# A hybrid attention layer on one core: the first feed-forward projection as seven block products for eight

## Chip, cores and metric

One core of one Trainium2 chip. The metric is the device time in microseconds of one execution of the program.

## What is computed

One layer on x of 512 tokens by 1024, all in fp32:

```python
h = rms_norm(x, g_mix)
proj = h @ w_in                    # q, k, v of two attentions, two gates
ya = moba_attention(...)           # 8 heads, blocks of 256
yb = swa_attention(...)            # 8 query heads, window 128, sinks
merged = sigmoid(ga) * (ya @ w_branch_a) + sigmoid(gb) * (yb @ w_branch_b)
x = x + merged @ w_out
h2 = rms_norm(x, g_ffn)
x = x + square(relu(h2 @ w_ff1)) @ w_ff2
```

w_ff1 is 1024 x 4096 and w_ff2 is 4096 x 1024. The change concerns the last line.

## The kernel before

Every fp32 product is made from three matmuls in the type fp32r. A matrix is split into a high part (ScalarE copies it into fp32r) and a low part (the matrix less its high part, on POOL or VectorE); high x high, high x low and low x high are summed in PSUM (`products`, L1382 to L1390).

**Stages.** Weights come in slabs of 128 x 1024 (512 KB). g numbers them: 18 of the QKV projection, 16 of the gates (their matmuls stand between the steps of attention), 8 of the branch projections, 8 of the output projection, then 32 of w_ff1 and 32 of w_ff2. The attention has 32 steps of two units each. In a step VectorE takes the maxima, ScalarE the exponentials, VectorE the reciprocals (L1118), and POOL normalises (L554); TensorE transposes them two steps later (L1554).

**A slab's way.** SP loads it into one of RAW = 4 slots of `w_raw` (`load_slab`, L421) once the low part of the slab four before is made. ScalarE makes `w_hi` (`split_hi`, L624, L630) once TensorE has freed one of WS = 2 slots, POOL makes `w_lo` (`split_lo`, L535, L538), TensorE runs 8 x 3 matmuls of 512 columns (L1387 to L1389).

**Feed-forward stage.** The 4096 hidden columns go in 8 chunks (CHUNKS) of 512, so of four slabs of w_ff1 (TILES = 4). `up(j, c)` (L1691) makes one tile of 128 hidden columns by 512 tokens with 24 matmuls; ScalarE applies Relu (L823) and square (L829). The second projection of a chunk is already done in Strassen's way, with PRODUCTS = 7 block products for 8 (`product`, L1711; its matmuls are L1705, L1707, L1708, 12 of 512 columns each). Their weight operands are blocks of w_ff2 or sums of blocks: VectorE makes four sums per chunk (`weight_sum_1` to `weight_sum_4`, L1203 to L1222), ScalarE the seven high parts (`down_hi`, L831, L842), VectorE four of the low parts (L1237) and POOL three (L594). Their other operands are blocks of the squared tiles or sums of them (L1248 to L1259), split by ScalarE (L850) and VectorE (L1242). VectorE adds the products to sums in `store` (L1270, L1280).

**Order.** Each engine has a written-out order, in one loop over the chunks (PE L1742, ACT L919, DVE L1304, POOL L618, SP L508); semaphores with counts tie them. TensorE runs, in chunk c, tiles 1, 2, 3 of the chunk and tile 0 of chunk c+1, then products 0 to 6:

```python
with pe.Fori(0, CHUNKS - 2) as c:
    for j in range(1, TILES + 1):
        up(j, c)
    for k in range(PRODUCTS):
        product(k, c)
```

Chunks 6 and 7 are written out with the tiles of chunk 7 between the products of 6. SP loads four slabs of w_ff1 per chunk (L487) and reloads four blocks of w_ff2 (L493) when their readers are done. No DMA is issued by POOL, and ScalarE issues two, at the start.

## Time and profile before

| | |
|---|---|
| median of 3 runs | 675.34 us (674.37 to 676.03) |
| profiled execution | 674.49 us |
| its span | 672.7 us |
| PE, PEld busy | 99%, 82% |
| DVE, ACT, POOL busy | 75%, 55%, 48% |
| DMA | 69.87 MB, 104 GB/s |

The profile covers one execution. PE is TensorE's matmuls and PEld its weight loads, which overlap them; DVE is VectorE. The span is a little shorter than the measured time. A matmul's end in the records is modelled and overlaps the next one, so the distance between two starts, not the mean duration, is what one costs. Engines work side by side: time on an engine off the path does not show in the total.

### The profile page before, as it was taken

How to read it: one execution, taken by the hardware profiler on the slowest of the kernel's cores; microseconds unless marked ns; L12 is line 12 of the kernel's file. 1: busy time of each engine (PE TensorE's matmuls, PEld its weight loads, DVE VectorE, ACT ScalarE, POOL GpSimd, SP SyncE). 2: the span in 40 equal slices, each digit the busy share in tenths (PEclk: the TensorE clock that was granted, in tenths of full speed). 3: DMA queues.
4: the chain of work that ended last, by engine and by line, in shares of the span. 5: the costliest groups of instructions: out<-in, count | busy, mean ns of one | idle time of the engine just before them, and what ended most of it. 6: DMA issues, size and time to landing. Idle time of an engine off the chain costs nothing.

```text
span 672.7 us, 9474 instructions
## 1 busy us (share of the span) xinstructions
PE 668.1 (99%) x3238; PEld 553.8 (82%) x3238; DVE 502.2 (75%) x701; ACT 371.1 (55%) x662; POOL 322.8 (48%) x194
## 2 busy tenths in 40 slices
PE   9999999999999999999999999999999999999998
PEld 7887788888888888888888888888888888888886
DVE  6668898555555555875559879787897888979797
ACT  7468677776666666534357546253553625536360
POOL 0256577466555662444445536246452444436532
PEclk9999999999999999999999999999999999999999
DMA  8222342222233113454222322315132151230303
GB/s 322 95 98 91 86 138 71 73 79 94 95 95 95 64 53 109 167 181 179 88 71 94 129 90 85 133 62 174 57 108 96 62 187 62 94 108 18 126 0 126
DMA packets 22909, 69.87 MB, mean 104 GB/s; under 512 B 2731, under 2 KB 4011, under 8 KB 22876
## 3 DMA queue, kind: packets, MB, share of 16 engines
q1 hardware_dynamic: 22588, 68.92, 30.4%
q10 hardware_dynamic: 288, 0.52, 0.2%
q8 instruction: 19, 0.31, 0.2%
q14 instruction: 14, 0.11, 0.1%
HBM read 67.27 MB, written 2.16 MB: 103 GB/s over the span
## 4 chain that ended last, share of the span: by engine, by line
PE 97%; ACT 1%; DMA 1%; POOL 0%; issue 0%; DVE 0%; SPq 0%; ACTq 0%
PE bank L1387 21%; PE bank L1389 21%; PE bank L1388 21%; PE bank L1708 8%; PE bank L1707 8%; PE bank L1705 8%; PE bank L1488 3%; PE bank L1538 2%; PE bank L1554 2%; PE bank L1575 1%; PE bank L1577 1%; DMA store<-x_t 1%; PE bank L1677 1%; PE bank L1415 0%; PE bank L1416 0%; POOL w_lo L538 0%
## 5 line engine op out<-in xcount | busy, mean ns | idle before, releaser
L538 POOL TENSOR_TENSOR w_lo<-w_raw,w_hi 128x1024 fp32r<-128x1024 f32 x77 | 190.5, 2479 | 232.2 <-ACT w_hi L630 228.0
L1387 PE MATMUL bank<-qk_hi,w_hi 128*128 128x512 f32 x320 | 125.0, 391 | 0.0
L1389 PE MATMUL bank<-qk_hi,w_lo 128*128 128x512 f32 x320 | 124.5, 389 | 0.0
L1388 PE MATMUL bank<-qk_lo,w_hi 128*128 128x512 f32 x320 | 124.5, 389 | 0.0
L1387 PE MATMUL bank<-x_hi,w_hi 128*128 128x512 f32 x304 | 122.4, 402 | 0.1
L1389 PE MATMUL bank<-x_hi,w_lo 128*128 128x512 f32 x304 | 118.8, 391 | 0.0
L1388 PE MATMUL bank<-x_lo,w_hi 128*128 128x512 f32 x304 | 118.4, 390 | 0.0
L630 ACT ACTIVATE w_hi<-w_raw 128x1024 fp32r<-128x1024 f32 x80 | 83.9, 1058 | 57.3 <-PE bank L1389 53.2
L1270 DVE SCALAR_TENSOR_TENSOR store<-bank,softmax,store 128x512 f32<-128x512 f32 x101 | 71.9, 744 | 22.9 <-PE bank L1708 22.8
L1708 PE MATMUL bank<-v_parts,x_lo 128*128 128x512 f32 (+1 forms) x218 | 84.4, 387 | 0.0
L1705 PE MATMUL bank<-v_parts,x_hi 128*128 128x512 f32 (+1 forms) x218 | 84.4, 387 | 0.0
L1387 PEld LDWEIGHTS bank<-qk_hi,w_hi 128*128 128x128 f32 x320 | 60.1, 188 | 12.5 <-DVE w_lo L1181 0.2
L1389 PEld LDWEIGHTS bank<-qk_hi,w_lo 128*128 128x128 f32 x320 | 60.1, 188 | 12.5
L1388 PEld LDWEIGHTS bank<-qk_lo,w_hi 128*128 128x128 f32 x320 | 60.1, 188 | 12.3
L1389 PEld LDWEIGHTS bank<-x_hi,w_lo 128*128 128x128 f32 x304 | 57.0, 188 | 12.6
L1387 PEld LDWEIGHTS bank<-x_hi,w_hi 128*128 128x128 f32 x304 | 57.1, 188 | 12.0 <-issue 0.9
L1388 PEld LDWEIGHTS bank<-x_lo,w_hi 128*128 128x128 f32 x304 | 57.2, 188 | 10.8
L554 POOL TENSOR_SCALAR probs<-probs,softmax 128x256 f32<-128x256 f32 (+3 forms) x64 | 30.9, 495 | 58.4 <-DVE softmax L1118 58.3
L1123 DVE TENSOR_TENSOR pt_lo<-bank,pt_hi 128x256 fp32r<-128x256 f32 (+3 forms) x64 | 27.9, 439 | 36.6 <-ACT pt_hi L753 36.4
L842 ACT ACTIVATE v_parts<-qk_lo_again 128x1024 fp32r<-128x1024 f32 x21 | 21.5, 1057 | 57.1 <-DVE qk_lo_again L1213 45.9
L1705 PEld LDWEIGHTS bank<-v_parts,x_hi 128*128 128x128 f32 x218 | 40.9, 188 | 8.4
L1708 PEld LDWEIGHTS bank<-v_parts,x_lo 128*128 128x128 f32 x218 | 40.9, 188 | 8.3
(165 smaller groups left out, 1211.4 us busy)
## 6 DMA issues: line engine op xcount, KB each, us to landing
w_raw<-slabs SPq DMA_DIRECT2D x80, 512.0 KB, 3.3
bias_m<-slabs SPq DMA_DIRECT2D x16, 512.0 KB, 3.6
qk_hi_again<-slabs SPq DMA_DIRECT2D x16, 512.0 KB, 5.0
store<-x_t SPq DMA_DIRECT2D x16, 256.0 KB, 4.0
bias_m<-tab_dram SPq DMA_DIRECT2D x8, 256.0 KB, 4.2
out<-store SPq DMA_DIRECT2D x7, 256.0 KB, 2.8
bias_m<-tab_dram SPq DMA_DIRECT2D x8, 128.0 KB, 3.9
w_raw<-slabs ACTq DMA_DIRECT2D x2, 256.0 KB, 3.4
```

What stands on the lines that cost most here:

```text
L538: pool.tensor_tensor(w_lo[:, g % WS, :], w_raw[:, g % RAW, :], w_hi[:, g % WS, :].bitcast(F32), ALU.subtract).then_inc(w_lo_ready, 1)
L554: pool.tensor_scalar(probs[:, u % 4, 0:n], probs[:, u % 4, 0:n], rec[:, u % 8:u % 8 + 1], 1.0, ALU.mult, ALU.mult).then_inc(probs_ready, 1)
L630: act.activation(w_hi[:, g % WS, :], w_raw[:, g % RAW, :], ACT.Copy).then_inc(w_hi_ready, 1)
L842: act.activation(high, from_, ACT.Copy).then_inc(unit_hi_ready, 1)
L1123: dve.tensor_tensor(pt_lo[:, slot(u), keys], bank[5 + e][:, keys], pt_hi[:, slot(u), keys].bitcast(F32), ALU.subtract).then_inc(pt_lo_read ...
L1270: dve.scalar_tensor_tensor(out=to, in0=product, scalar=factor(j, m), in1=to, op0=ALU.mult, op1=ALU.add).then_inc(ready, 1)
L1387: pe.matmul(out_, wh, xh, start=first, stop=False)
L1388: pe.matmul(out_, wh, xl, start=False, stop=False)
L1389: last = pe.matmul(out_, wl, xh, start=False, stop=end)
L1705: pe.matmul(to, u_high, high[:, p, cols], start=(opens and p == 0), stop=False, skip_group_check=True)
L1707: pe.matmul(to, u_high, low[:, p, cols], start=False, stop=False, skip_group_check=True)
L1708: last = pe.matmul(to, u_low, high[:, p, cols], start=False, stop=(p == 1), skip_group_check=True)
```

## The change

Chunk 0's up projection stays as it was (three tiles after the one before). In chunks 1 to 7 the product of w_ff1's 1024 x 512 part with the 512 tokens is done as a 2 x 2 block product in Strassen's way (Winograd's form), with seven block products (UPS). The contraction is halved into even and odd tiles, the tokens into two halves (NEAR, FAR), the hidden columns into two halves. One block product is 2 x 4 x 3 = 24 matmuls of 256 columns.

- **Token operands.** While the output projection runs, ScalarE scales x1 (`scaled_x1`), VectorE makes four sums of half tiles per pair of tiles (`half_sums`), and both split them into `sum_hi` and `store_low`. They serve all chunks.
- **Weight sums.** The sums of weight blocks for both projections are made in DRAM (`sum_dram`): a DMA copies a block (28 issued by ACT, 32 by SP), and accumulating DMAs issued by POOL add another block or sum. There are 15 sets (chunk and projection) of four sums: 60 copies and 60 accumulating DMAs of 512 KB. The copies are issued from the QKV stage on; one accumulating DMA per step of attention, then two per slab. VectorE's weight sums go, and SP loads seven blocks per projection and chunk for four.
- **Low parts.** Of the seven up blocks, four low parts are made by POOL (0, 4, 5, 6); for blocks 1, 2, 3 (ADDED_UPS) ScalarE writes the negated high part and an accumulating DMA from POOL adds the fp32 block to it. Of the down products VectorE makes 1, 2, 3 and POOL 0, 4, 5, 6.
- **Order.** TensorE runs the seven up blocks of chunk c and then its products in the order 0, 2, 1, 3, 4, 5, 6; nothing of chunk c+1 stands ahead of them. For the last chunk the up blocks stand between products 4 and 5 of the chunk before.
- **After a block.** The blocks add up in banks 7 and 6 in part, and in SBUF in part: VectorE adds banks to tiles (`up_product`, five per chunk), ScalarE copies block 0 out (`first_up_copy`), and applies Relu and square to four results.

Core of the diff (the rest follows from it: counts of semaphores, slots, host arrangement of w_ff1):

```diff
+SUM_ORDER = [(SETS[n - back], s) for n in range(len(SETS) + 1) for back, s in ((0, S1), (1, S2), (0, S3), (1, S4))
+             if 0 <= n - back < len(SETS)]
...
# SP
+            def copy_down(n):
+                at, s = COPY_DOWNS[n]
+                sp.dma_start(set_at(at)[s], block_of(at, COPIED["down"][s])).then_inc(copy_done[at], 16)
...
                 load_slab(g)
+                if 0 <= g - COPIES_BEHIND < len(COPY_DOWNS):
+                    copy_down(g - COPIES_BEHIND)
...
+            for c in range(CHUNKS):
+                more = c + 1 < CHUNKS
+                if c == 0:
+                    sp.wait_ge(slab_done, G_FF + TILES)
+                    for k in (4, 5):
+                        load_up(k, 1)
+                if more:
+                    next_down(3, c)
+                    next_down(2, c)
+                if c and more:
+                    next_up(0, c)
+                if c:
+                    sp.wait_ge(up_done, up_count(1, c))
+                    load_up(6, c)
+                sp.wait_ge(b_lo_ready, c * len(B_UNITS) + 1)
+                load_down(6, c)
+                if more:
+                    next_down(1, c)
+                if c and more:
+                    for k in (2, 3, 4, 5, 1):
+                        next_up(k, c)
+                if more:
+                    next_down(4, c)
+                    next_down(5, c)
+                    next_down(0, c)
...
# POOL
+            def add_to_sum(n):
+                if n >= len(SUM_ORDER):
+                    return
+                at, s = SUM_ORDER[n]
+                if s in (S1, S3):
+                    pool.wait_ge(copy_done[at], 64 if at == ("up", 1) else 128)
+                    src = block_of(at, ADDED[at[0]][s])
+                else:
+                    pool.wait_ge(sum_done[at], 32 if s == S2 else 48)
+                    src = set_at(at)[S1 if s == S2 else S2]
+                pool.dma_start(set_at(at)[s], src, accum_op=ALU.add,
+                               max_dma_last_dim=4 * D).then_inc(sum_done[at], 16)
...
+                if step >= 1:
+                    add_to_sum(step - 1)
...
-            for g in range(LATE + 2, G_FF + 3):
+            for g in range(LATE + 2, G_FF + TILES):
                 split_lo(g, g + 3)
+                for n in range(2):
+                    add_to_sum(STEPS + 2 * (g - LATE - 2) + n)
...
+            def up_add(k, c):
+                at = ("up", c)
+                src = block_of(at, UP_BLOCK[k]) if k in UP_BLOCK else set_at(at)[UP_SUM[k]]
+                pool.wait_ge(up_minus_ready, (c - 1) * len(ADDED_UPS) + ADDED_UPS.index(k) + 1)
+                pool.dma_start(w_low[:, RAW_SLOT[k], :], src, accum_op=ALU.add).then_inc(up_added[k], 16)
...
                 down_lo(0, c)
+                if c:
+                    for k in (4, 5, 6):
+                        up_lo(k, c)
+                up_lo(0, c + 1)
+                down_lo(4, c)
...
+                    down_lo(5, c)
+                    up_add(2, c + 1)
+                    down_lo(6, c)
+                    up_add(1, c + 1)
+                    up_add(3, c + 1)
...
# ACT
             for g in range(N_VA, N_QKV):
                 split_hi(g + 2)
+                copy_up(g - N_VA)
...
+            def chunk(c):
+                down_hi(3, c)
+                down_hi(2, c)
                 down_hi(0, c)
                 down_hi(1, c)
+                first_up_copy(c)
+                up_hi(4, c)
+                up_hi(5, c)
+                up_relu(0, c)
+                up_square(0, c)
+                up_hi(6, c)
+                u_part_hi(6, c)
+                up_hi(0, c + 1)
+                up_relu(1, c)
+                up_square(1, c)
+                u_part_hi(0, c)
+                up_relu(2, c)
+                up_square(2, c)
+                u_part_hi(2, c)
+                up_relu(3, c)
+                up_square(3, c)
+                u_part_hi(1, c)
+                u_part_hi(3, c)
+                down_hi(4, c)
+                u_part_hi(4, c)
+                u_part_hi(5, c)
+                next_splits(c)
...
# DVE
+            def chunk_start(c):
+                for k in T_UNITS:
+                    down_lo(k, c)
+                up_product(1, c)
+                up_product(3, c)
+                u_part_lo(6, c)
+                up_product(4, c)
+                up_product(5, c)
+                u_part_lo(0, c)
+                u_sum_1(c)
+                up_product(6, c)
+                u_sum_2(c)
+                u_part_lo(2, c)
+                u_part_lo(1, c)
+                add_both(0, c)
+                u_sum_3(c)
+                u_part_lo(3, c)
+                u_sum_4(c)
+                u_part_lo(4, c)
+                add_both(2, c)
+                add_both(1, c)
+                u_part_lo(5, c)
+                add_both(3, c)
+                add_both(4, c)
...
# PE, in up(k, c)
+                for n in range(2):
+                    to = out_[:, S // 2 * n:S // 2 * n + S // 2]
+                    for i in range(KT // 2):
+                        high, low = up_weight(k, i, n)
+                        x_high, x_low = up_moving(k, i)
+                        pe.matmul(to, high, x_high, start=(k in UP_OPENS and n == 0 and i == 0), stop=False,
+                                  skip_group_check=True)
+                        pe.matmul(to, high, x_low, start=False, stop=False, skip_group_check=True)
+                        last = pe.matmul(to, low, x_high, start=False, stop=(i == KT // 2 - 1), skip_group_check=True)
...
-            with pe.Fori(0, CHUNKS - 2) as c:
-                for j in range(1, TILES + 1):
-                    up(j, c)
-                for k in range(PRODUCTS):
+            with pe.Fori(1, CHUNKS - 2) as c:
+                ups(c)
+                for k in ORDER:
                     product(k, c)
```

## Rows read from the trace of the kernel before

**Rows 1.** The page: span, busy time of each engine, the chain that ended last.

```profile
span 672.7 us, 9474 instructions
PE   668.1 (99%) x3238; PEld 553.8 (82%) x3238; DVE 502.2 (75%) x701; ACT 371.1 (55%) x662; POOL 322.8 (48%) x194
...
PE 97%; ACT 1%; DMA 1%; POOL 0%; issue 0%; DVE 0%; SPq 0%; ACTq 0%
```

**Rows 2.** Busy time by stretch, with granted clock, DMA share and GB/s.

```profile
core 0: us, PE busy (x) PEld busy (x) DVE busy (x) ACT busy (x) POOL busy (x), PEclk, DMA share, GB/s
0.00:25.00 25.00, 23.78 (x103) 20.22 (x104) 17.41 (x33) 16.10 (x23) 2.21 (x8) 1.00 0.73 259
25.00:120.00 95.00, 95.00 (x433) 76.92 (x433) 75.50 (x92) 66.49 (x114) 58.38 (x30) 1.00 0.30 95
...
433.00:474.00 41.00, 41.00 (x183) 33.95 (x182) 34.35 (x34) 19.47 (x26) 18.76 (x7) 1.00 0.30 102
```

**Rows 3.** Timeline of VectorE, one chunk apart: start, duration, instruction.

```profile
430.12 0.75 DVE L1270 SCALAR_TENSOR_TENSOR store<-bank,softmax,store 128x512 f32<-128x512 f32 x1 [0.61 <-PE bank L1708]
...
470.92 0.75 DVE L1270 SCALAR_TENSOR_TENSOR store<-bank,softmax,store 128x512 f32<-128x512 f32 x1 [0.61 <-PE bank L1708]
```

**Rows 4.** Timeline of the end of the kernel, PE, PEld and DVE.

```profile
664.07 0.39 PE L1707 MATMUL bank<-pt_hi,x_hi 128*128 128x512 f32 x1
...
667.69 0.39 PE L1708 MATMUL bank<-v_parts,x_lo 128*128 128x512 f32 x1
...
667.92 0.28 PE L1705 MATMUL bank<-v_parts,x_hi 128*128 128x256 f32 x1
...
668.03 0.28 PE L1707 MATMUL bank<-v_parts,x_hi 128*128 128x256 f32 x1
668.04 0.19 PEld L1708 LDWEIGHTS bank<-v_parts,x_lo 128*128 128x128 f32 x1
...
669.23 0.28 PE L1708 MATMUL bank<-v_parts,x_lo 128*128 128x256 f32 x1
669.55 0.48 DVE L1377 SCALAR_TENSOR_TENSOR store<-bank,softmax,store 128x256 f32<-128x256 f32 x1 [0.16 <-PE bank L1708]
```

**Rows 5.** Groups of instructions by form, 390 to 630 us: busy, mean ns.

```profile
L630 ACT ACTIVATE w_hi<-w_raw 128x1024 fp32r<-128x1024 f32 x24 | 24.6, 1051 | 0.0
L1237 DVE TENSOR_TENSOR pt_hi<-qk_lo_again,v_parts 128x1024 fp32r<-128x1024 f32 x18 | 21.4, 1218 | 7.3 <-ACT v_parts L842 7.3
L1222 DVE TENSOR_TENSOR qk_lo_again<-qk_hi_again,qk_lo_again 128x1024 f32<-128x1024 f32 x6 | 20.5, 3422 | 0.0
L594 POOL TENSOR_TENSOR pt_hi<-qk_hi_again,v_parts 128x1024 fp32r<-128x1024 f32 x6 | 20.4, 3402 | 0.0
L594 POOL TENSOR_TENSOR v_parts<-bias_m,v_parts 128x1024 fp32r<-128x1024 f32 x6 | 14.4, 2399 | 26.5 <-ACT v_parts L842 26.5
L1242 DVE TENSOR_TENSOR x_lo<-probs,x_hi 128x512 fp32r<-128x512 f32 x24 | 29.2, 1236 | 0.0
L823 ACT ACTIVATE probs<-bank 128x512 f32<-128x512 f32 x24 | 14.3, 594 | 16.8 <-PE bank L1389 16.7
L1280 DVE TENSOR_TENSOR pt_lo_again<-bank,pt_lo_again 128x512 f32<-128x512 f32 x12 | 7.7, 683 | 0.0
L1213 DVE TENSOR_TENSOR qk_lo_again<-qk_hi_again,qk_lo_again 128x1024 f32<-128x1024 f32 x6 | 7.4, 1226 | 0.3
L1217 DVE TENSOR_TENSOR bias_m<-qk_hi_again,bias_m 128x1024 f32<-128x1024 f32 x6 | 7.3, 1219 | 0.0
L1207 DVE TENSOR_TENSOR qk_lo_again<-bias_m 128x1024 f32<-128x1024 f32 x6 | 7.3, 1217 | 0.0
```

**Rows 6.** Timeline of a chunk, VectorE and then ScalarE.

```profile
449.61 0.69 DVE L1257 TENSOR_TENSOR x_lo_again<-probs 128x512 f32<-128x512 f32 x1
...
450.34 0.64 ACT L850 ACTIVATE x_hi<-x_lo_again 128x512 fp32r<-128x512 f32 x1 [2.63 <-DVE x_lo_again L1257]
```

**Rows 7.** The page: DMA queue (share of 16 engines) and issues with time to landing.

```profile
q1 hardware_dynamic: 22588, 68.92, 30.4%
...
w_raw<-slabs SPq DMA_DIRECT2D x80, 512.0 KB, 3.3
bias_m<-slabs SPq DMA_DIRECT2D x16, 512.0 KB, 3.6
qk_hi_again<-slabs SPq DMA_DIRECT2D x16, 512.0 KB, 5.0
```

**Rows 8.** Tile w_raw: ns of one DMA issue (min/median/max) on SP and ACT.

```profile
L429 SPq DMA_DIRECT2D w_raw<-slabs x55: 327/328/517, 7.2 to 352.3; - x55
...
L412 ACTq DMA_DIRECT2D w_raw<-slabs x1: 413/413/413, 0.7 to 0.7; - x1
```

**Rows 9.** Timeline of a slab of the output stage: ScalarE, POOL, TensorE.

```profile
312.58 1.06 ACT L630 ACTIVATE w_hi<-w_raw 128x1024 fp32r<-128x1024 f32 x1 [3.63 <-PE bank L1389]
...
313.72 2.40 POOL L538 TENSOR_TENSOR w_lo<-w_raw,w_hi 128x1024 fp32r<-128x1024 f32 x1 [3.53 <-ACT w_hi L630]
...
318.58 0.48 PE L1387 MATMUL bank<-x_hi,w_hi 128*128 128x512 f32 x1
```

**Rows 10.** Waits: who waited for whom, us in total, times, longest.

```profile
POOL probs L554 <- DVE softmax L1118: 58.3, 23, 5.0
```

**Rows 11.** Busy time by stretch, two slabs of the output stage.

```profile
312.67:318.58 5.91, 5.91 (x31) 4.90 (x30) 3.07 (x3) 2.16 (x4) 2.40 (x1) 1.00 0.49 180
...
324.51:330.43 5.92, 5.92 (x32) 4.90 (x30) 3.08 (x3) 2.17 (x4) 2.40 (x1) 1.00 0.27 94
```

More of the change, by code:

```diff
@@ L616, in last_lows @@
                 down_lo(5, c)
-            with pool.Fori(0, CHUNKS - 1) as c:
+            for c in range(CHUNKS - 1):
                 chunk_lows(c)
@@ new lines, in relu, with square, up_hi @@
+            def relu(j):
+                act.wait_ge(slab_done, G_FF + j + 1)
+                act.activation(u_raw[:, j, :], bank[7 - j % 2][:, :], ACT.Relu).then_inc(relu_ready, 1)
+            def square(j):
+                act.wait_ge(relu_ready, j + 1)
+                u = u_raw[:, j, :]
+                act.activation(u, u, ACT.Square).then_inc(u_ready, 1)
+            def up_hi(k, c):
+                slot = RAW_SLOT[k]
+                if k < 4:
+                    if isinstance(c, int) and c == 1:
+                        act.wait_ge(slab_done, G_FF + TILES)
+                    else:
+                        act.wait_ge(up_done, up_count((4, 5, 6, 3)[k], c - 1))
+                else:
+                    act.wait_ge(up_done, up_count(k - 4, c))
+                act.wait_ge(up_arrived[slot], up_arrived_count(k, c))
+                act.activation(quarters(up_high[HIGH_SLOT[k]]), up_raw(slot), ACT.Copy).then_inc(up_hi_ready, 1)
@@ L1699, in product_part, with ups @@
+            def ups(c):
+                for k in range(UPS):
+                    up(k, c)
             def product_part(k, m, out_, high, low, cols, opens):
```

628 lines of the change are left out of this document (404 added, 224 removed).

## The prediction

> **What bounds the kernel now.** I read the page's first part and its chain first [rows 1]: TensorE is busy 99% of a 672.7 us span, and 97% of the chain that ended last is matmul. The profiled execution took 674.49 us, 1.8 us more than its span and 0.85 us less than the median of the three runs (675.34), so my sums are made against 674.5 and 0.85 us is added at the end. Then the windows by stage [rows 2]: in a chunk of the feed-forward stage VectorE works 34.4 of 41 us, ScalarE 19.5, POOL 18.8 and the DMA engines are 30% busy. The clock is granted in full (1.00, the 2.4 GHz level) in every stretch. The timeline of the chunk loop [rows 3] gives the period: the same VectorE addition starts at 430.12 and at 470.92, 40.80 us apart. A chunk has 96 matmuls of the up projection and 84 of the down products; 40.80/180 = 0.2267 us each, which is the distance of back-to-back 512-column matmuls at the end of the kernel [rows 4], where 664.07 to 667.69 is 16 of them. So the loop has no PE gap at all: any PE time taken out shows in full, as long as nothing else becomes late, and nothing that relieves another engine pays anything.
>
> **What the change takes out.** Chunks 1 to 7 lose 7 x 96 = 672 matmuls of 512 columns and gain 7 blocks x 24 = 168 matmuls of 256 columns each, 1176. The price of one with 256 columns stands in the last product of the kernel [rows 4]: from 668.03 to 669.23 are ten steps, 0.120 us, not the half of 0.2267 (0.113). The weight load (0.19 us there as elsewhere) overlaps the matmuls before it and does not stretch this. Removed: 672 x 0.2267 = 152.3 us. Added: 1176 x 0.120 = 141.1 us; with the 0.119 that the whole group gives (667.92 to 669.23 in 11 steps), 140.1. I take **11.7 us less** PE time. 674.5 - 11.7 = 662.8.
>
> The Trainium skill (TensorE: Matmul & The Clock Gate, Back-to-back issue gap) gives the gap as columns over 2.4 GHz plus 2.5 ns, that is 109 and 216 ns. By that page the exchange would be 145.0 against 128.4 us and save 16.6. The trace has 120 and 227 ns for this kernel's operands, so the rows decide.
>
> **What must stay hidden in a chunk.** The new period is 40.80 - 1.67 = 39.1 us.
> - ScalarE: before, 11 copies of 1024 elements and 15 passes of 512, at 1.05 and 0.6 us [rows 5]; after, 17 and 16, about 28 of 39.1 us. Hidden.
> - VectorE: the four weight sums go (1.22 + 1.23 + 1.22 + 3.42 = 7.1 us) and one of four low parts (1.2); five additions from PSUM come (5 x 0.69) [rows 5]. 34.4 - 8.3 + 3.5 = 29.6. Hidden, and worth nothing by itself.
> - POOL: eight subtractions for seven, 2.4 us alone and up to 3.4 when VectorE is in its way [rows 5], and three accumulating DMAs. At most 27 us plus the issues. Hidden on average.
> - DMA: 17 transfers of 512 KB for eight. In the first 25 us the engines are 73% busy at 259 GB/s [rows 2], so full use is 355 GB/s and 512 KB cost 1.5 us of all 16: 25 us of 39.1, up to 30 if an accumulating one costs double. Busy, not full.
>
> **Latencies at the chunk's start.** Before, the first tile of chunk c+1 stood ahead of the products of chunk c (24 x 0.2267 = 5.4 us of cover). Now products follow the seven blocks at once. Product 0 needs only block 4. Product 2, second in the new order, needs block 5: let block 5 end at 0. VectorE starts 0.2 us after a matmul's successor could (669.23 + 0.12 to 669.55 [rows 4]); hops between engines are 0.05 (449.61 + 0.69 to 450.34 [rows 6]). Addition 0.9, Relu 1.5, square 2.2, S1 2.9, its high part 3.6. VectorE has meanwhile queued block 6's addition, which waits for that block (2.86): 3.75, then S2: 4.5, then the low part of S1: 5.2. PE wants it after block 6 and product 0, at 2.86 + 2.72 = 5.58. It fits by 0.4 us. Product 1 (its parts ready at about 6.5, wanted at 8.3) and product 3 fit by more. Block 2's wait for the copy of block 0 out of its bank has 2.86 us for a 0.6 us copy. I put these at nothing, with up to 0.5 us a chunk (3.5 in all) as the upper end. PE takes its work in order, so a miss is a gap.
> The queues of a chunk: SP loads the raw block 6 once block 1 has freed its slot, at 5.7, so that it lands at 9 to 10.7 (3.3 to 5.0 us [rows 7]); its two parts take 1.05 and up to 3.4 us, and PE wants them at 17.2. POOL issues the accumulating DMA of the next block 1 behind the low part of product 6, at about 35 us of 39.1; block 1 is wanted 2.9 us into the next chunk, at 42.0, so it may take 6.6 us. Both are hidden.
>
> **The weight sums in DRAM.** This is the part that no row of before shows. 60 copies and 60 accumulating DMAs of 512 KB are added, and with 66 more loads in the feed-forward stage the traffic grows by 186 x 1.5 = 279 us of all engines, to 204 (30.4% of the span [rows 7]) + 279 = 483 of 660; doubled accumulates (81) make it about 600. The queues:
> - Issue on ACT costs 0.42 us, on SP 0.33 [rows 8]. ACT: 14 in the QKV stage, one per 5.4 us slab, where it idles 30%, and 14 in attention, one per two steps. Hidden. SP's 32 copies stand between slab loads, each loaded up to four slabs ahead and landing in 3.3 us [rows 7]; a copy ahead of it adds some 1.5 to 3 us. Hidden.
> - Issue on POOL has no row: nothing to 1.7 us, the latter being half of the 3.5 us that POOL idles per slab in the output stage [rows 9]; beyond it PE waits. I take about 1 us, nearer ACT's row than the end. In attention POOL waited 58 us for VectorE's reciprocals, 2.5 us a time [rows 10], and the issue stands there. Hidden; up to 1 us in total is allowed where it isn't.
> - Landing time of an accumulate: from 3.3 us (a load [rows 7]) to about 8 (5.0, the slowest row for 512 KB, and a second read at 1.5, doubled by traffic). POOL itself waits for the one two places earlier. In attention two places are two steps, over 10 us. From the branch stage on there are two per slab, so POOL may wait once an accumulate needs more than a slab's 5.4 to 5.9 us. What stands behind that wait is the low part of the slab weights, ready only 2.5 us before PE takes it (313.72 + 2.40 against 318.58 [rows 9]). I take 4.8 us, one load and one more read: hidden.
> - The extra ScalarE and VectorE work in the output stage (eight scaled copies, twelve sums) goes into 3.5 us idle per slab on ScalarE [rows 9]. Nothing.
>
> The sum: 662.8, plus 1.4 for small gaps (0.2 us in each of seven chunks, under half of the bound) = 664.2; plus 0.85 for the median: **665.0**. A measurement of this kernel can tell about 0.3%, 2 us, from no change.
>
> **Rivals.**
> 1. *The accumulates in DRAM are late (slower).* The place is the 16 slabs of the branch and output stages and the first up tiles. Per slab the engines have 0.27 to 0.49 of 5.92 us in use already [rows 11]; two accumulates at 1.5 us bring that to 4.6 to 5.9, at 3.0 us (reading both terms) to 7.6 to 8.9. It decides from 5.9 us a slab and makes the kernel slower than before (677.4, the 0.3% included) from 6.8. At 7.0 it costs 1.1 x 16 = 18 us: 662.8 + 0.85 + 18 = 682; at 6.5 half of that, 673. For it: the sums leave no slack once doubled. Against: loads share the engines with the POOL queue, and slab loads land four slabs ahead. Chance 0.27 that it is slower by this.
> 2. *The shared port makes the new chain miss (gain partly lost).* One VectorE subtraction of 1024 took 3.42 us beside POOL's, and 1.23 alone; one of 512 from the u tiles 1.24 on average instead of 0.68 [rows 5]. If a POOL subtraction lies over the 5.2 us chain, product 2 is 2.0 us late, in seven chunks 14 us: 678, a bit slower; if it does so only in part, 0.5 to 1 us a chunk, 667 to 671. Against: by the order on POOL its next-chunk subtraction ends before block 5 does and the following one waits for product 0. Chance 0.15, most of it for the partial case.
> The Trainium skill (SBUF — State Buffer, SBUF: two separate sides) calls this an exclusive lock held for a whole instruction, with DMA descriptors from POOL shut out as well. The trace agrees for POOL's subtractions; no row of before has a DMA from POOL.
> 3. *The copies saturate the DMA engines in the QKV stage,* so slabs and bias tiles come late at the start of attention: 24 copies in 76 us make 36 us on top of 30% (23 us), 78% in use; at double price for writing DRAM, 125%. Then some 5 to 10 us are lost there, 670 to 675. Chance 0.08.
> 4. Forecast, all of it hidden but for 3 us: chance 0.50.
>
> **Numbers.** The likeliest case gives 665, its own range 662.5 to 668. The other cases reach upward: the range is 662 to 682. Faster by over 0.3% takes the forecast, most of 3 and the partial part of 2: 0.63. Within 0.3%: 0.10. Slower: 0.27.
>
> **What would show it.** Right: up blocks of 24 matmuls in 2.86 us, a chunk period of 39.1, no PE idle before the up blocks or products, stages before the feed-forward stage ending when they did. Rival 1: PE idle before slab matmuls released by POOL's w_lo in the branch and output stages, and POOL waiting for a DMA. Rival 2: PE idle before product 2 released by VectorE's x_lo. Rival 3: gaps before 200 us behind a load. The forecast is wrong if the 256-column step is over 0.13 us, since 0.01 us more costs 12 us.

## The result, and the profile after

The changed kernel takes 735.63 us (median of 4 runs, 734.69 to 736.81) against 675.68 for the kernel before on the same chip: ratio **1.0885** (95% interval 1.0866 to 1.0903), 60 us slower. The forecast was 665.0, faster, and its range ended at 682. The profiled execution has a span of 732.8 us.

The page of the kernel after: span, engines, TensorE clock and DMA in 40 slices of 18.3 us, queues (packets, MB, share of 16 engines), the chain that ended last.

```profile
span 732.8 us, 10654 instructions
PE 682.2 (93%) x3742; PEld 581.0 (79%) x3742; DVE 480.9 (66%) x719; ACT 426.7 (58%) x723; POOL 401.8 (55%) x282
...
PEclk9999999997999999989899999999999999999799
DMA  8487698999999997999997677593949577585503
...
q1 hardware_dynamic: 35468, 109.29, 42.4%
q0 software_dynamic: 11664, 42.47, 31.0%
q10 hardware_dynamic: 1184, 15.21, 5.3%
...
PE 41%; DMA 31%; POOL 12%; DVE 7%; ACT 4%; issue 4%; DVEq 0%; ACTq 0%; SPq 0%
```

Against [rows 1] the chain has left TensorE: it was 97% PE, it is 41%, and 31% is DMA. The DMA digits of the slices 6 to 21 are 8 and 9 but for one. Queue 0 is POOL's: it carries the 81 accumulating DMAs (60 in DRAM, 21 into SBUF) and nothing else. 0.310 x 732.8 / 81 = **2.8 us of all 16 engines each**. A transfer in q1 (109.29 MB are 208 of 512 KB, loads and SP's 32 copies) costs 0.424 x 732.8 / 208 = 1.49, and q10, ScalarE's queue, carries 28 copies at 0.053 x 732.8 / 28 = 1.39.

Busy time by stretch (PE, PEld, DVE, ACT, POOL, then granted clock, DMA share of 16 engines, GB/s), kernel after:

```profile
25.00:120.00 95.00, 95.00 (x428) 76.83 (x429) 75.24 (x93) 66.13 (x114) 60.14 (x31) 1.00 0.76 260
120.00:290.00 170.00, 157.47 (x942) 130.04 (x941) 87.23 (x263) 100.05 (x269) 108.50 (x120) 0.97 1.00 268
290.00:345.00 55.00, 47.02 (x195) 37.69 (x194) 29.16 (x29) 21.33 (x29) 30.32 (x24) 0.94 1.04 256
345.00:392.00 47.00, 40.93 (x177) 32.97 (x176) 26.73 (x28) 22.16 (x31) 22.16 (x17) 0.93 1.02 235
433.00:474.00 41.00, 40.29 (x256) 36.26 (x255) 32.46 (x34) 26.12 (x33) 23.55 (x11) 1.00 0.68 208
```

The QKV stage (25 to 120) has the DMA engines at 0.76, where [rows 2] had 0.30, and still no PE gap. From 120 to 392 they are full (1.00 to 1.04), and PE idles 12.5, 8.0 and 6.1 us. These 26.6 us are not the whole loss: the granted clock in the three rows is 0.97, 0.94 and 0.93, so up to 0.03 x 170 + 0.06 x 55 + 0.07 x 47 = 11.7 us more lie in matmuls that ran at the lower level (1.2 GHz) after gaps. The last row is 41 us of the feed-forward loop, a little over one chunk, against the 433 to 474 of [rows 2]: VectorE down, ScalarE and POOL up, and 0.7 us of PE idle.

The waits of the kernel after (who waited for whom: us in total, times, longest), then the group of POOL's issues that stand behind them, then from the page the issues with their time to landing:

```profile
POOL sum_dram L712 <- DMA sum_dram<-sum_dram: 84.9, 14, 9.0
...
PE bank L1725 <- POOL w_lo L676: 25.5, 14, 4.9
PE bank L2072 <- DMA w_raw<-sum_dram: 6.7, 6, 2.4
PE bank L2089 <- DVE pt_lo_again L1576: 4.5, 1, 4.5
```

```profile
L712 POOL DMA_DIRECT2D sum_dram<-sum_dram x30 | 31.2, 1041 | 86.8 <-DMA sum_dram<-sum_dram 84.9
```

```profile
w_raw_again<-slabs SPq DMA_DIRECT2D x66, 512.0 KB, 6.6
...
sum_dram<-slabs POOLq DMA_DIRECT2D x30, 512.0 KB, 10.9
sum_dram<-sum_dram POOLq DMA_DIRECT2D x30, 512.0 KB, 10.5
```

POOL waits 84.9 us for its own accumulates, which land 10.5 to 10.9 us after issue (medians of the whole run; 12.4 and 12.7 for those issued in attention, from 120 to 255 us). The low part of the slab weights (L676) stands behind that wait, and PE behind the low part. A weight load that took 3.3 us [rows 7] now takes 6.6. POOL's timeline in the output stage shows it in one place (start, duration, instruction, idle before and its releaser):

```profile
300.62 0.80 POOL L712 DMA_DIRECT2D sum_dram<-slabs  x1
307.43 0.83 POOL L712 DMA_DIRECT2D sum_dram<-sum_dram  x1 [6.00 <-DMA sum_dram<-sum_dram]
307.97 2.66 POOL L676 TENSOR_TENSOR w_lo<-w_raw_again,w_hi 128x1024 fp32r<-128x1024 f32 x1
```

and PE takes that low part up 2.77 us late:

```profile
310.69 0.64 PE L1725 MATMUL bank<-qk_hi,w_hi 128*128 128x512 f32 x1 [2.77 <-POOL w_lo L676]
```

It is the same everywhere: each of PE's 15 gaps between 140 and 400 us comes 1 to 5 us after the end of one of POOL's 14 waits for a landing.

**Where the 60 us are.** Starts of matmuls in the trace, in us after the kernel's first matmul; e1 is the first experiment, without the sums in DRAM:

| | before | after | e1 |
|---|---|---|---|
| last scores of attention | 236.7 | 253.0 | 238.0 |
| first transpose ahead of the feed-forward slabs | 305.5 | 333.7 | 306.9 |
| last of these transposes | 347.3 | 385.8 | 348.6 |
| first product of chunk 0 | 369.2 | 408.0 | 365.1 |
| last product | 668.1 | 728.6 | 686.2 |

Against e1, 42.9 us are lost ahead of the first product (15 in attention, 12 more by the first transpose, so in the branch stage and the first two slabs of the output stage, 10 in the rest of the output stage, 6 in the slabs after it). The feed-forward stage itself is no shorter than before. By blocks: chunk 0's products take 26.5 us instead of 19.0, the seven up blocks of chunks 1 to 6 take 21.0 to 21.4 where 168 steps of 0.120 are 20.15, the last chunk's 31.1, and the products in the loop 19.46 instead of 19.04. That is 7.5 + 6.6 + 10.9 + 2.5 = 27.5 us. 42.9 + 27.5 less the forecast gain of 11.7 is 58.7 of the 60.5. Chunk 0's products and the last chunk's up blocks, in the columns of the table by stretch:

```profile
408.92:435.43 26.51, 21.22 (x86) 16.76 (x85) 22.86 (x29) 16.73 (x20) 12.37 (x7) 0.94 0.71 210
674.18:705.28 31.10, 24.98 (x169) 24.43 (x168) 15.52 (x14) 13.26 (x17) 18.80 (x9) 0.84 0.43 114
```

PE idles 5.3 and 6.1 us in them; the lower granted clock (0.94 and 0.84) takes up to 1.6 and 5.0 us more.

### The profile page after: what moved, and what is told of

It is laid out like the page before. It is cut to its first block, busy times and chain, and to the rows that moved or that the text cites. A ratio compares the mean times of both kernels' runs of the same rounds, so it can differ in the third digit from the quotient of the medians.

```text
span 732.8 us, 10654 instructions
## 1 busy us (share of the span) xinstructions
PE 682.2 (93%) x3742; PEld 581.0 (79%) x3742; DVE 480.9 (66%) x719; ACT 426.7 (58%) x723; POOL 401.8 (55%) x282
## 3 DMA queue, kind: packets, MB, share of 16 engines
q1 hardware_dynamic: 35468, 109.29, 42.4%
q0 software_dynamic: 11664, 42.47, 31.0%
## 4 chain that ended last, share of the span: by engine, by line
PE 41%; DMA 31%; POOL 12%; DVE 7%; ACT 4%; issue 4%; DVEq 0%; ACTq 0%; SPq 0%
DMA sum_dram<-sum_dram 22%; PE bank L2072 5%; DMA w_raw<-sum_dram 5%; PE bank L1725 5%; PE bank L2075 5%; PE bank L2074 5%; PE bank L1726 5%; PE bank L1727 5%; POOL w_lo L676 5%; POOL pt_hi L760 4%; PE bank L1826 3%; DMA sum_dram<-slabs 3%; POOL sum_dram L712 2%; DVE x_hi_again L1544 2%; PE bank L2089 2%
## 5 line engine op out<-in xcount | busy, mean ns | idle before, releaser
L676 POOL TENSOR_TENSOR w_lo<-w_raw_again,w_hi 128x1024 fp32r<-128x1024 f32 x49 | 129.1, 2642 | 68.7 <-ACT w_hi L808 65.0
L1725 PE MATMUL bank<-x_hi,w_hi 128*128 128x512 f32 x304 | 125.5, 413 | 18.4 <-POOL w_lo L676 18.4
L808 ACT ACTIVATE w_hi<-w_raw_again 128x1024 fp32r<-128x1024 f32 x52 | 55.1, 1060 | 75.3 <-PE bank L1727 71.7
L1725 PEld LDWEIGHTS bank<-x_hi,w_hi 128*128 128x128 f32 x304 | 58.7, 193 | 33.4 <-POOL w_lo L676 21.1
L712 POOL DMA_DIRECT2D sum_dram<-sum_dram x30 | 31.2, 1041 | 86.8 <-DMA sum_dram<-sum_dram 84.9
L1566 DVE SCALAR_TENSOR_TENSOR store_again<-bank,softmax,store_again 128x512 f32<-128x512 f32 x101 | 70.0, 742 | 11.4 <-PE bank L2092 11.4
L1561 DVE TENSOR_TENSOR probs<-bank,probs 128x512 f32<-128x512 f32 x35 | 24.1, 690 | 59.4 <-PE bank L2075 47.0
L2072 PE MATMUL bank<-sum_hi,w_hi 128*128 128x256 f32 x168 | 48.9, 291 | 6.7 <-DMA w_raw<-sum_dram 6.7
L937 ACT ACTIVATE pt_hi<-bank 128x256 fp32r<-128x256 f32 (+3 forms) x64 | 22.1, 395 | 53.4 <-PE bank L1892 53.1
L2075 PE MATMUL bank<-qk_hi,w_raw 128*128 128x256 f32 x168 | 48.6, 289 | 0.0
L2074 PE MATMUL bank<-store,w_hi 128*128 128x256 f32 x168 | 48.2, 287 | 0.0
L2091 PE MATMUL bank<-pt_hi,x_hi 128*128 128x512 f32 x120 | 46.7, 389 | 0.0
## 6 DMA issues: line engine op xcount, KB each, us to landing
sum_dram<-slabs POOLq DMA_DIRECT2D x30, 512.0 KB, 10.9
sum_dram<-sum_dram POOLq DMA_DIRECT2D x30, 512.0 KB, 10.5
```

Of the source, the lines that this page charges most:

```text
L676: pool.tensor_tensor(w_lo[:, g % WS, :], w_raw[:, g % RAW, :], w_hi[:, g % WS, :].bitcast(F32), ALU.subtract).then_inc(w_lo_ready, 1)
L808: act.activation(w_hi[:, g % WS, :], w_raw[:, g % RAW, :], ACT.Copy).then_inc(w_hi_ready, 1)
L1566: dve.scalar_tensor_tensor(out=to, in0=product, scalar=factor(j, m, minus), in1=to, op0=ALU.mult, op1=ALU.add).then_inc(ready, 1)
L1725: pe.matmul(out_, wh, xh, start=first, stop=False)
L2072: pe.matmul(to, high, x_high, start=(k in UP_OPENS and n == 0 and i == 0), stop=False, skip_group_check=True)
L2074: pe.matmul(to, high, x_low, start=False, stop=False, skip_group_check=True)
```

## The experiments

The theories after the result: **A**, the accumulates fill the DMA engines and POOL waits for them; it explains only the part ahead of the products. **B**, something else costs in these stages (copies, issues). And for the 27.5 us: late pieces in the first and last chunk, and the add into block 1. Kernels that leave the sums out load a plain block in place of each sum, so they do the work of the transfers and not the computation. The edits are shown in their core lines, against the kernel after, those of h2 and h3 against h1.

**e1, no sums.** The 60 copies and 60 accumulates are out, and each load of a sum takes a plain block.

```diff
-                sp.dma_start(set_at(at)[s], block_of(at, COPIED["down"][s])).then_inc(copy_done[at], 16)
+                pass
...
-                    src = set_at(at)[DOWN_SUM[k]]
+                    src = block_of(at, COPIED["down"][DOWN_SUM[k]])
```

> Leaves out the 60 copies and the 60 accumulating DMAs that make the sums in DRAM; the loads take a plain block from the weights instead, so the weight sums are missing from the result. Everything else, the three accumulating DMAs into SBUF per chunk too, is as in the changed kernel. Theory A (the 16 DMA engines are full before the feed-forward stage: 107 us of old traffic + 60 x 1.4 + 60 x 2.8 = 359 us of demand before 386 us): the stages up to the last x1 transpose end as before (347 us after the first matmul, not 386), and the gaps at the start of the feed-forward stage (13 us) go too: 735.6 - 38.6 - 13 = about 684. Theory B (the extra ScalarE, VectorE and POOL work and the new orders cost the time, not the DMAs): at least 720.

**e2, copies only.** As e1, but the 60 copies run and are loaded in place of the sums; the adds are left out.

```diff
-                pool.dma_start(set_at(at)[s], src, accum_op=ALU.add,
-                               max_dma_last_dim=4 * D).then_inc(sum_done[at], 16)
+                return
```

> The 60 copies stay, the 60 accumulating DMAs are left out, so the sums hold one block each. Theory A: demand 107 + 84 = 191 us of 350, so within 3 us of the kernel without sums, about 685. Rival (the DRAM to DRAM copies delay slabs and bias tiles in the QKV stage and attention): 10 us or more above the kernel without sums.

**e3, no chain.** The second sum of each set adds to a plain block, so that every add waits for copies alone (the sums are other ones than the reference's).

```diff
-                if s in (S1, S3):
-                    pool.wait_ge(copy_done[at], 64 if at == ("up", 1) else 128)
-                    src = block_of(at, ADDED[at[0]][s])
-                else:
-                    pool.wait_ge(sum_done[at], 32 if s == S2 else 48)
-                    src = set_at(at)[S1 if s == S2 else S2]
+                pool.wait_ge(copy_done[at], 64 if at == ("up", 1) else 128)
+                src = block_of(at, ADDED[at[0]][s] if s in (S1, S3) else COPIED[at[0]][s])
```

> All copies and all accumulating DMAs stay, but the second and fourth sum add a block of the weights instead of the sum made just before, so POOL has no accumulating DMA to wait for, only copies; those sums are not the right ones. Theory A (engines full): the traffic is the same, so the stages before the feed-forward stage stay late by 25 us or more; total 715 to 740. Rival C (not the traffic but POOL's waits for landings in its own order cost the time): these waits are gone, 684 to 690.

**e5, plain copies for adds.** Same queue, same waits and same bytes, without the addition (each sum is overwritten by its second block).

```diff
-                pool.dma_start(set_at(at)[s], src, accum_op=ALU.add,
-                               max_dma_last_dim=4 * D).then_inc(sum_done[at], 16)
+                pool.dma_start(set_at(at)[s], src).then_inc(sum_done[at], 16)
```

> The 60 accumulating DMAs into DRAM become plain copies of the same size, from the same queue with the same waits; the sums hold a copied block. Theory A: a 4 KB packet takes 328 ns when it accumulates and 159 ns when not, so the demand falls from 359 to 275 us and is no longer full: 684 to 695. Rival C (landing order): POOL still waits for each, so over 710. Rival D (the issue of a DMA by POOL, 1 us of its time, is the price): unchanged, 725 to 736.

**e7, up's sums only.** 28 copies and 28 adds instead of 60 and 60; down's sums are left out.

```diff
+                if at[0] == "down":
+                    return
```

> The changed kernel with the 28 copies and 28 accumulating DMAs of the up projection alone; the sums of the down projection are left out (plain blocks in their place). Theory A (full engines): demand before the feed-forward stage 107 + 28 x 1.4 + 28 x 2.8 = 224 of 350 us, nothing is full, so within 2 us of the kernel without any sums: 692 to 694. Rival C (each accumulating DMA makes POOL wait, whatever the load): half of the 44 us stay, about 713.

| | us | ratio to before (95%) |
|---|---|---|
| after | 735.63 | 1.0885 (1.0866 to 1.0903) |
| e3 no chain | 718.34 | 1.062 (1.0491 to 1.0749) |
| e7 up's sums only | 694.41 | 1.0292 (1.0253 to 1.0331) |
| e2 copies only | 694.27 | 1.0264 (1.0186 to 1.0343) |
| e5 adds as plain copies | 693.37 | 1.0251 (1.0177 to 1.0326) |
| e1 no sums | 691.66 | 1.0226 (1.0146 to 1.0306) |

Windows of e3, then of e5, 120 to 290 and 290 to 345, then POOL's queue on the page of e5:

```profile
120.00:290.00 170.00, 162.69 (x966) 136.34 (x963) 91.62 (x267) 102.70 (x273) 111.73 (x123) 0.97 1.00 275
290.00:345.00 55.00, 50.42 (x222) 40.92 (x221) 37.84 (x33) 24.88 (x34) 34.61 (x27) 0.97 1.06 266
```

```profile
120.00:290.00 170.00, 169.90 (x1018) 142.27 (x1017) 100.24 (x275) 109.83 (x284) 108.49 (x130) 1.00 0.84 302
290.00:345.00 55.00, 55.00 (x258) 45.42 (x257) 41.09 (x39) 26.71 (x37) 31.26 (x31) 1.00 0.93 344
```

```profile
q0 software_dynamic: 4944, 42.47, 20.0%
```

Taking the sums out gives 44 us back (e1 was expected at 684, 8 us lower), and the copies are within 3 us of nothing. Without the chain of waits (e3, whose two runs took 715.4 and 721.3) 17 of the 44 come back, and the engines are still full at 1.00 and 1.06: the waits cost, and full engines cost without them. With plain copies in place of the adds (e5) the same waits and the same number of POOL issues stay, the engines come to 0.84 and 0.93, and PE idles for 0.10 us in 170. So the chain of waits alone does no harm; with the price of accumulating it does. In e5 queue 0 costs 0.200 x 691.9 = 138 us; less 21 adds into SBUF at 2.8 (e1's queue 0, which has these alone: 0.084 x 690.8 / 21) it leaves 1.3 us for each of the 60, where an add costs 2.8. Two reservations. e5 also moves larger packets (4944 in queue 0 instead of 11664). But in the kernel after a packet of 4096 B takes 328 ns (median) in queue 0, where it is added, and 159 ns in q1, where it is only moved, so size doesn't make the double price. And an issue holds POOL for a mean of 0.52 us in e5 instead of 1.11. No run holds that apart; for the landing as the cause speaks that each gap of PE follows a wait for one. e7 halves the adds, its engines reach 0.71 and 0.88, and it costs nothing ahead of the first product: the demand fits into the stages there, and nothing is late.

**The 28 us left.** e1 is free of DRAM sums and is still 26 us over the forecast's sum for it (677.3 - 11.7 = 665.6). Its TensorE waits from 363 us on:

```profile
PE bank L2063 <- DMA w_raw<-slabs: 7.9, 6, 2.8
PE bank L2080 <- DVE pt_lo_again L1567: 4.5, 1, 4.5
```

The 4.5 us stand in chunk 0, once. VectorE there in e1, and POOL at the same time:

```profile
373.65 0.16 DVE L1592 TENSOR_SCALAR softmax<-softmax 128x4 f32<-128x4 f32 x1
...
374.06 2.31 DVE L1596 TENSOR_SCALAR softmax<-softmax 128x4 f32<-128x4 f32 x1
376.29 0.41 DVE L1478 TENSOR_TENSOR store_again<-store_again 128x256 f32<-128x256 f32 x1
376.62 2.56 DVE L1479 TENSOR_TENSOR store_again<-store_again 128x256 f32<-128x256 f32 x1
...
379.89 1.28 DVE L1567 TENSOR_TENSOR pt_lo_again<-bank,pt_lo_again 128x512 f32<-128x512 f32 x2
```

```profile
373.95 2.39 POOL L744 TENSOR_TENSOR w_raw<-w_raw_again,w_hi 128x1024 fp32r<-128x1024 f32 x1 [11.23 <-ACT w_hi L1034]
376.30 2.59 POOL L751 TENSOR_TENSOR v_parts<-qk_lo_again,v_parts 128x1024 fp32r<-128x1024 f32 x1
```

An instruction of four columns takes 2.31 us because a POOL subtraction runs from 373.95 to 376.34, and a half sum at 376.62 is held by the next subtraction in the same way. Both stand ahead of the addition of product 0 that frees its bank. The 7.9 us in six waits are the add of block 1, in chunks 2 to 6 and (2.8 us) in the last. In the kernel after its issue, for chunk 3, starts at 512.83 and PE, which wants it at 519.8, gets it at 520.62:

```profile
512.83 1.23 POOL L747 DMA_DIRECT2D w_raw<-sum_dram  x1
```

```profile
520.62 0.39 PE L2072 MATMUL bank<-sum_hi,w_hi 128*128 128x256 f32 x1 [0.84 <-DMA w_raw<-sum_dram]
```

It takes 7.8 us from issue to use.

**e4, block 1 first.** e1 with block 1's parts and its add ahead of block 2's, in all chunks.

```diff
-UP_HI_ORDER = [0, 2, 1, 3, 4, 5, 6]
-ADDED_UPS, UP_LOWS = (2, 1, 3), (0, 4, 5, 6)
+UP_HI_ORDER = [0, 1, 2, 3, 4, 5, 6]
+ADDED_UPS, UP_LOWS = (1, 2, 3), (0, 4, 5, 6)
```

> The kernel without sums in DRAM (691.7 us), in which the parts of block 1 are now made before those of block 2: its accumulating DMA into SBUF is issued one subtraction (2.4 to 3.4 us) earlier. Theory E (in the chunk loop block 1 waits 1.0 to 1.6 us for the landing of that DMA, which takes 7.9 us and not the 6.6 that I allowed): the gap goes in six chunks and shrinks in the last, 691.7 - 8 = about 684, and the up blocks of a chunk take 20.1 to 20.3 us instead of 21.3. Rival F (the DMA queues are busy, so whichever block is second in line waits): the gap moves to block 2 and the time stays at 690 to 692.

**e8, a quarter of the add.** e1 with 256 of the 1024 columns accumulated into SBUF (the rest of the sum is left out).

```diff
-                pool.dma_start(w_low[:, RAW_SLOT[k], :], src, accum_op=ALU.add).then_inc(up_added[k], 16)
+                pool.dma_start(w_low[:, RAW_SLOT[k], 0:D // 4], src[:, 0:D // 4], accum_op=ALU.add).then_inc(up_added[k], 16)
```

> The kernel without sums in DRAM, in which the three accumulating DMAs into SBUF of each chunk add only the first 256 of 1024 columns, so that most of three low parts is wrong; order and waits are the same. Theory E: the landing falls by the transfer time of three quarters (2.1 us of all engines each) and the gap at block 1 goes, 684. Rival (the issue on POOL or the copies on ScalarE are late, not the landing): unchanged, 691.

**e6, chunk 0's order.** e4, and in chunk 0 the four half sums that stood just ahead of product 0's addition are made earlier, while VectorE waits for a square; in the last chunk block 0's copy out of its bank comes ahead of a high part.

```diff
                 u_part_lo(4, c)
+                half_sums(3)
                 u_sum_1(c)
...
                 dve.tensor_scalar(r2_minus, r2, -1.0, None, ALU.mult).then_inc(r2_ready, 1)
-                half_sums(3)
```

> As the run before, and in chunk 0 VectorE makes the last four half sums while it waits for the third square instead of ahead of the additions of product 0; in the last chunk ScalarE copies block 0 out before it splits a block of the second projection. Theory G (in chunk 0 TensorE idles 4.6 us because bank reads stand behind those four sums, and then runs at the half clock for a while; the chunk's products take 28.4 us for 19.0): about 9 us less than the run before, and 1 to 2 us less in the last chunk: 673. Rival (the idle time comes from the reciprocals and their waits, which stay): 682.

**e9, the last chunk's order.** e6, and in the last chunk the parts of down weight 0 come behind the parts of up blocks 4, 5 and 6, on ScalarE (shown) and POOL.

```diff
-                down_hi(0, c)
                 first_up_copy(c)
...
                 up_hi(6, c)
+                down_hi(0, c)
                 down_hi(3, c)
```

> As the run with chunk 0 mended (no sums in DRAM, 680.8 us), and in the last chunk ScalarE splits the first block of the second projection, whose load lands late, behind the parts of up blocks 4, 5 and 6 instead of ahead of them; POOL's order follows. Theory H (TensorE's wait of 6.8 us before block 4 of chunk 7, and the half clock behind it, come from ScalarE standing at that load): the last up blocks take 20 to 21 us instead of 29.3, so 672. Rival (block 4's raw block itself lands late): unchanged at 680.

| | us | ratio (95%) | chunk 0 products | up blocks, loop | up blocks, last | products, last |
|---|---|---|---|---|---|---|
| e1 | 691.66 | 1.0226 (1.0146 to 1.0306) | 28.4 | 21.3 | 29.1 | |
| e4 | 688.2 | 1.0200 (1.0171 to 1.0230) | 28.4 | 20.15 | 31.3 | |
| e8 | 688.25 | 1.0201 (1.0172 to 1.0231) | | 21.05 | 29.7 | |
| e6 | 680.79 | 1.0088 (1.0029 to 1.0147) | 23.2 | 20.15 | 29.3 | 24.7 |
| e9 | 675.33 | 1.0004 (0.9988 to 1.0019) | 23.1 | 20.15 | 20.5 | 29.7 |

The intervals of e1, e4 and e8 overlap, so what these three show is read from the times of the blocks. In e4 the gap ahead of block 1 is gone and the loop's period is 20.15 + 19.46 = 39.6 us, where the forecast had 39.1. The run is only 3.5 us shorter and missed its 684, since the last chunk's wait grew. The waits of e4 from 363 us on:

```profile
PE bank L2063 <- ACT probs L1050: 7.7, 1, 7.7
PE bank L2080 <- DVE pt_lo_again L1567: 4.5, 1, 4.5
```

e8 removes the landing wait too, but its up blocks are only 0.25 us shorter than e1's: in each chunk of the loop PE now waits ahead of block 3. That is not for block 3's add, which landed at 473.37 in this chunk, but for VectorE, which must first add block 1 out of the bank that block 3 writes:

```profile
473.96 3.43 DVE L1514 TENSOR_TENSOR pt_hi<-qk_hi_again,v_parts 128x1024 fp32r<-128x1024 f32 x1
477.31 3.43 DVE L1514 TENSOR_TENSOR pt_hi<-bias_m,v_parts 128x1024 fp32r<-128x1024 f32 x1
480.67 0.68 DVE L1552 TENSOR_TENSOR probs<-bank,probs 128x512 f32<-128x512 f32 x1
```

```profile
481.40 0.39 PE L2063 MATMUL bank<-sum_hi,w_lo 128*128 128x256 f32 x1 [0.65 <-DVE probs L1552]
```

Both low parts, the second and third of the chunk, take 3.43 us instead of 1.22, each beside a POOL subtraction (473.33 to 476.30 and 476.66 to 479.66). A cheaper add alone uncovers VectorE held beside POOL, the mechanism of rival 2, as the next limit. In e4 POOL works later, the second low part takes 1.22 us and the third 2.72, and PE doesn't wait.

e6 and e9 take up the two rows above in turn: chunk 0 gives 5.2 us, the last chunk's up blocks 8.8. e6 was expected at 673 and came to 680.8: chunk 0 still idles 3.3 us, at a granted clock of 1.00 (6.1 us at 0.88 in e1), and the last chunk's wait stayed at 6.6 us. e9 was expected at 672 and came to 675: its last products are 5 us longer, because the low part of an activation (VectorE's x_lo) is late now and the clock falls behind the gap (0.94 in this stretch):

```profile
PE bank L2080 <- DVE x_lo L1519: 3.1, 1, 3.1
```

(In e9 one chunk of the loop has a gap of 0.9 us besides.) So even with the DRAM sums out and the orders mended the exchange only reaches the kernel before.

**Complete versions.** Since 28 adds fit (e7) and 60 don't, three kernels compute the whole with up's sums in DRAM and down's four sums on VectorE as before, with e9's orders.

**h1**, the first of them (its core; the loads of the four plain blocks and the waits follow from it):

```diff
+            def weight_sum(n, c):
...
+                dve.tensor_tensor(to, a, b, ALU.add).then_inc(t_ready, 1)
...
                 add_both(0, c)
+                weight_sum(4, c)
                 u_sum_3(c)
```

> A complete kernel: the up projection as in the changed kernel with its 28 copies and 28 accumulating DMAs into DRAM, but the four sums of the down projection per chunk made by VectorE as before, with the orders of the run above. Theory A: demand on the DMA engines 224 of 350 us before the feed-forward stage, so nothing is lost there; the chunk loop at 39.6 us a chunk if VectorE's four additions (4 x 1.22 us) find room. Total about 673, a little faster than the kernel before. Rival I (POOL and VectorE hold their shared port 19.2 + 16.1 = 35.3 of 39.6 us, so the new chain of blocks misses): gaps of 1 us or more in each chunk, 680 or more.

**h2** moves the fourth weight sum (and in the last chunk two low parts):

```diff
                 add_both(0, c)
-                weight_sum(4, c)
                 u_sum_3(c)
...
                 add_both(2, c)
+                weight_sum(4, c)
                 add_both(1, c)
```

> The whole computation, as in h1_hybrid: up's sums made in DRAM (28 copies, 28 adds), down's four sums made by VectorE in SBUF. Three edits of VectorE's order alone: the fourth weight sum stands behind the adds of products 0 and 2 instead of ahead of them (chunks 0 to 6), and in the last chunk the low parts of activations 2 and 1 stand ahead of the adds of products 5 and 6 of the chunk before. A (VectorE's order is what is left): h1_hybrid's chunk 0 products took 28.9 us with gaps of 2.6 and 4.25, its chunks 1 to 6 a gap of about 1.0 each ahead of product 3, its last chunk's products 28.2 with a gap of 3.4. With the sum out of the way chunk 0 gives back 4 to 5, the chunks 1 to 6 some 6 together, the end 2 to 3: 691.9 - 13 = 679, so still not below the kernel before at 675. B (VectorE is full, or the port that it shares is, so that a gap only moves to the next low part): 688 to 692.

**h3** puts it where VectorE idles (and in the last chunk moves six scalings back and two low parts forward):

```diff
                 down_lo(1, c)
+                weight_sum(4, c)
                 up_product(3, c)
```

> The whole computation, as in h1_hybrid, but the fourth weight sum stands among the up products, where h1_hybrid's VectorE idles (2.3 us ahead of the addition of up block 3), not among the adds that free the product banks; in the last chunk the six scalings of the common sum go behind the additions of the up products, and the low parts of activations 2 and 1 ahead of the adds of products 5 and 6 of the chunk before. A (a weight sum costs nothing in a place where VectorE idles, 3.5 us where a bank waits behind it, as h2_hybrid_reordered's gaps of 3.47 show): no gap in chunks 1 to 6, 6 us below h1_hybrid, 3 more in chunk 0, 2 to 3 at the end: 691.9 - 11 = 681, above the kernel before. B (the place only moves the gap): 690 or more.

Measured: h1 691.94 (ratio 1.0251, 1.0220 to 1.0282), h2 712.87 (1.0573, 1.0540 to 1.0606), h3 689.44 (1.0229, 1.0206 to 1.0252). h1 missed its 673: in each chunk of its loop PE waits 0.85 us for VectorE's x_lo and the products take 20.6 us instead of 19.5, as its rival had it, and chunk 0's take 28.9. h2 went past both of its cases. VectorE and then TensorE in h2:

```profile
469.01 3.30 DVE L1533 TENSOR_TENSOR bias_m<-qk_hi_again,bias_m 128x1024 f32<-128x1024 f32 x1
472.24 1.40 DVE L1582 SCALAR_TENSOR_TENSOR store_again<-bank,softmax,store_again 128x512 f32<-128x512 f32 x2
```

```profile
473.03 0.80 PE L2121 MATMUL bank<-v_parts,x_hi 128*128 128x512 f32 x1 [3.33 <-DVE store_again L1582]
473.63 0.63 PE L2123 MATMUL bank<-v_parts,x_hi 128*128 128x512 f32 x1
474.05 0.63 PE L2124 MATMUL bank<-v_parts,x_lo 128*128 128x512 f32 x1
```

The moved sum lies beside a POOL subtraction (468.86 to 471.23) and takes 3.30 us instead of 1.23; the additions behind it free the product's bank, and PE stands 3.3 us in every chunk. After that its matmuls are 0.43 us apart instead of 0.227. The windows of h2 before, in and after this gap:

```profile
466.00:469.00 3.00, 3.00 (x15) 2.44 (x14) 3.00 (x5) 2.43 (x4) 0.14 (x1) 1.00 0.00 0
469.70:473.00 3.30, 0.01 (x1) 0.00 (x0) 3.30 (x3) 1.55 (x3) 2.34 (x2) 0.98 0.13 10
473.10:476.00 2.90, 2.90 (x7) 2.33 (x8) 2.46 (x5) 2.90 (x4) 2.42 (x1) 0.50 0.93 179
476.50:480.00 3.50, 3.50 (x17) 2.88 (x16) 1.60 (x3) 1.84 (x2) 1.67 (x2) 1.00 1.12 404
```

The granted clock is 0.50, the 1.2 GHz level, for about 3 us after PE stood for 3.3, then 1.00 again. Seven matmuls at 0.43 add 1.4 us to the gap; a chunk's products take 24.2 us in h2 against 20.6 in h1. h3 has no wait on VectorE over 0.5 us in the loop and a period of 40.3 against 40.76, but its last products have a gap of 5.5 us in place of h1's 3.3, and chunk 1's up blocks one of 2.9. It gains 2.5 us of the 11 expected. No version run here that computes the whole is faster than the kernel before.

## Why the prediction was wrong

- **Removed and added matmuls: right.** The up step of 256 columns is 0.120 us (168 in 20.15 us wherever nothing is late, in e4, h1 and e9), and the period without waits is 39.6 against the forecast 39.1; the 0.5 comes almost wholly from the products, 19.46 for 19.04. The Trainium skill (TensorE: Matmul & The Clock Gate, Back-to-back issue gap) gives 109 ns, by which an estimate for the 168 matmuls is 18.3 us. The 20.15 here do not bear that out.
- **Failed step 1: "I take 4.8 us, one load and one more read: hidden."** An accumulate in DRAM landed after 10.5 to 10.9 us, above even the bound of 8, and POOL waited 84.9 us in total. The bound was made from loads on engines that were 30% busy.
- **Failed step 2, the reason for it: the sum was made for the whole span.** The total of 483 us of 660, about 600 with doubled accumulates, was right in size: 42.4 + 31.0 + 5.3 = 79% of 732.8 is 577. But all the sums lie ahead of 393 us. From 120 to 290 there are 32 adds and 29 copies issued: 49 (0.29 x 170, the share of before there) + 32 x 2.8 + 29 x 1.4 = about 180 us of engines in 170 us. The text gave both prices, 1.5 and 3.0 us, and went on with the lower. In e5, where these transfers cost the lower one, nothing ahead of the products is late.
- **Rival 1 was the mechanism, with place and size too small.** It named the two steps seen: POOL waiting for a DMA, and PE released by w_lo. At its upper price it had 7.6 to 8.9 us per slab, that is 1.7 to 3.0 late in each of 16, up to 48 us, and then took 7.0. It left out attention, where 15 of the 42.9 us are lost, because two places there are over 10 us: the accumulates landed there after 12.4 to 12.7 us.
- **Rival 3 was wrong.** The QKV stage came to 0.76 (78% was worked out) and lost nothing; e2's copies cost within 3 us of nothing.
- **Rival 2 was right in mechanism, in another place.** Product 2 was on time in the loop. But beside POOL VectorE was held 2.31 and 2.56 us in chunk 0 of e1, 3.30 in h2, and twice 3.43 in e8's loop, where block 3 waited for it. The Trainium skill (SBUF — State Buffer, SBUF: two separate sides) speaks of a lock for a whole instruction; the 128x4 instruction that ends with POOL's subtraction agrees.
- **Failed step 3: "so it may take 6.6 us. Both are hidden."** The forecast of the place was right (issue 4 us before the chunk's start), the time was 7.8 from issue to use: a wait of 0.7 to 0.95 us in each of the chunks 2 to 6 and 2.4 in the last. e4 removed it by order alone.
- **Failed step 4: the first and last chunk weren't looked at.** "0.2 us in each of seven chunks" treats all alike. 18.4 us lie in chunk 0's products and the last up blocks, each with its own order on VectorE and ScalarE. The last up blocks wait 2.4 us for block 1's add, 2.9 for ScalarE and 0.8 for VectorE's additions. e6 and e9 took 14 us out there by order, against e1, and e9's last products then gave 5 back. Part of each loss is the clock: no term of the prediction had a price for the lower level after a gap, 0.84 granted in the last up blocks.
- The busy times of a chunk came out as worked out: VectorE 28.8 us, ScalarE 26.1, POOL 22.7 (475.92 to 516.74), for 29.6, 28 and at most 27. SP's copies and the raw block 6 cost nothing, as said. The one wait of PE in the loop that names VectorE's new additions is 0.64 us in chunk 1.

What stays open: the order that mends the last chunk without a late product; why the loop's products take 19.46 instead of 19.04; a version with up's sums in DRAM and no gap at either end, which from h3 would have to find 15.5 us more to pass the kernel before; and how much of the loss ahead of the products would stay if an issue held POOL as briefly as in e5.

## What to carry to other kernels

Sum what a change asks of the DMA engines for each stage, at the dearer of two prices that you can't tell apart, and if a stage comes out over its length, forecast the loss there instead of hiding it under the mean. A row that shows an engine idle says nothing of what queues behind a wait placed on it: list who stands behind. Where a loop is bound by TensorE with no gap, a saving of 2 us a chunk is smaller than one late piece in the chunks that are written out by hand, so walk through the first and last one by one.

## What the runs showed of the hardware

- A DMA that accumulates in DRAM or into SBUF costs 2.8 us of all 16 engines for 512 KB where a load costs 1.49 and a copy 1.39. It landed after 10.5 to 10.9 us with full engines (12.4 to 12.7 in attention); the same transfers without the addition landed after 5.9 to 6.8 in e5.
- Issuing one in DRAM held POOL for 0.80 to 1.71 us (mean 1.04 and 1.18 for the two kinds), and a plain copy in e5 for 0.49 to 0.74. ScalarE's copies took 0.50 to issue, SP's 0.81 (median), SP's loads about 0.33.
- While POOL subtracted, VectorE was held even in an instruction of 128x4: 2.31 us instead of 0.16 (e1).
- TensorE's clock was granted at 0.50 for about 3 us after a 3.3 us gap in h2, where the gap cost 1.4 us more than itself. The mean over the whole kernel after was 0.972, against 1.00 before.
